# A mixture of experts in a transformer kernel: token rows gathered pair by pair inside the expert loop

## The reference, cut to what matters

```python
# h2 = rms_norm(x) * (1 + sc_f) + sh_f, then for n = 512 tokens:
g_prob = softmax(h @ w_group + b_group);  g_top, g_idx = top_k(g_prob, 1)      # 4 groups
e_prob = softmax(expert logits of that group)                                 # 8 experts in it
e_top, e_idx = top_k(e_prob, 2)
w = g_top * e_top / sum(e_top)                                                # gates of 2 experts a token
for e in range(32):                                                           # D_EXPERT = 256
    a = silu(h @ w_gate_e[e]) * (h @ w_up_e[e])
    y = y + gates[:, e] * (a @ w_down_e[e])
out = x + g_f * y                                                             # then a layer norm
```

## Time and profile before

| | us |
|---|---|
| median of 3 runs (2051.89 to 2058.57) | 2056.76 |
| the profiled execution's own time | 2054.31 |
| its span, first to last instruction | 2052.5 |
| PE busy of the span | 1844.0 (90%) |
| DVE busy | 915.1 (45%) |
| ACT busy | 622.2 (30%) |
| POOL busy | 162.3 (8%) |

### The profile page before, as it was taken

One profiled execution on the slowest core, in us unless ns is written; L12 is line 12 of the kernel. 1 busy time (PEld: TensorE's weight loads), 2 busy tenths in 40 slices (PEclk: granted clock), 3 DMA queues, 4 the chain that ended last, 5 costly groups with the idle time before them and its releaser, 6 DMA issues. The chain is left out here.

```text
span 2052.5 us, 23756 instructions
## 1 busy us (share of the span) xinstructions
PE 1844.0 (90%) x8688; PEld 1262.0 (61%) x8692; DVE 915.1 (45%) x1646; ACT 622.2 (30%) x1121; POOL 162.3 (8%) x239
## 2 busy tenths in 40 slices
PE   4997996587776899999999999988999999999996
PEld 2444644423222556676788878865557678888785
DVE  3787823511102687682322223347866522222234
ACT  2024521110001225742333322223376223333222
POOL 1000000200000242010000000004500100000001
PEclk9999998799888899999999999999999999999998
DMA  9162034499995500032233342250002203334231
GB/s 377 75 246 83 1 126 164 176 420 421 421 422 199 207 1 13 10 119 57 62 102 89 95 143 82 86 196 1 1 22 114 62 23 100 102 94 151 72 93 42
DMA packets 146334, 270.38 MB, mean 132 GB/s; under 512 B 9344, under 2 KB 106624, under 8 KB 132672
## 3 DMA queue, kind: packets, MB, share of 16 engines
q1 hardware_dynamic: 142208, 259.44, 34.9%
q0 software_dynamic: 4032, 9.69, 1.3%
HBM read 260.72 MB, written 13.11 MB: 133 GB/s over the span
## 5 line engine op out<-in xcount | busy, mean ns | idle before, releaser
L278 PE MATMUL bank<-ht_hi,gate_up_hi 128*128 128x512 f32 x704 | 274.1, 389 | 3.1 <-ACT arena L1429 3.1
L280 PE MATMUL bank<-ht_hi,gate_up_lo 128*128 128x512 f32 x704 | 273.9, 389 | 0.0
L279 PE MATMUL bank<-ht_lo,gate_up_hi 128*128 128x512 f32 x704 | 273.9, 389 | 0.0
L2410 PE MATMUL bank<-arena 128*128 128x512 f32 (+3 forms) x640 | 197.1, 467 | 8.2 <-ACT arena L1276 5.6
L2410 PEld LDWEIGHTS bank<-arena 128*128 128x128 f32 x640 | 115.3, 197 | 84.6 <-issue 67.4
L2054 DVE TENSOR_TENSOR arena<-arena,bank 128x512 f32 (+1 forms) x44 | 30.2, 687 | 272.2 <-ACT arena L1295 272.2
L278 PEld LDWEIGHTS bank<-ht_hi,gate_up_hi 128*128 128x128 f32 x704 | 132.1, 188 | 31.3 <-issue 3.9
L280 PEld LDWEIGHTS bank<-ht_hi,gate_up_lo 128*128 128x128 f32 x704 | 132.1, 188 | 27.7
L279 PEld LDWEIGHTS bank<-ht_lo,gate_up_hi 128*128 128x128 f32 x704 | 132.1, 188 | 27.2
L278 PE MATMUL bank<-down_hi,product_hi 128*128 128x512 f32 x352 | 138.2, 393 | 3.5 <-DVE arena L2054 3.5
L280 PE MATMUL bank<-down_hi,product_lo 128*128 128x512 f32 x352 | 138.1, 392 | 0.0
(11 more groups left out here) (373 smaller groups left out, 2938.0 us busy)
## 6 DMA issues: line engine op xcount, KB each, us to landing
gate_up_whole<-w_gu SPq DMA_DIRECT2D x88, 512.0 KB, 5.1
arena<-w_gate_e SPq DMA_DIRECT2D x33, 1024.0 KB, 20.1
arena<-w_up_e SPq DMA_DIRECT2D x33, 1024.0 KB, 23.4
arena<-w_down_e SPq DMA_DIRECT2D x33, 1024.0 KB, 23.2
down_whole<-w_down SPq DMA_DIRECT2D x44, 512.0 KB, 3.5
arena<-w_ada SPq DMA_DIRECT2D x5, 4096.0 KB, 21.2
arena<-w_in SPq DMA_DIRECT2D x4, 2048.0 KB, 16.0
w_o_whole<-w_o SPq DMA_DIRECT2D x2, 4096.0 KB, 13.1
```

What stands on the lines that cost most here:

```text
L278: pe.matmul(ps, xh, wh, start=start, stop=False)
L279: pe.matmul(ps, xh, wl, start=False, stop=False)
L280: return pe.matmul(ps, xl, wh, start=False, stop=stop)
L2410: ins = pe.matmul(ps[:, 0:b - a], HT[:, c, t * P:(t + 1) * P], w_in2[j][:, c], start=c == 0, stop=c == C8 - 1)
```

## The change

It does these things.

- The sorted list goes: no second destination, no eight gathers ahead of the loop, no XsT, no windows. Only the slot layout is left, computed by `mark_places`, and one table (`take_table`) gives, for each slot, its token (`from_token`), its row in `expert_rows` (`to_row`) and its weight (`w_slot`). The table for the 16 pairs is made first; that for the extras inside the loop, at pair 0 (DVE, `extra_rows`) and pair 1 (PE).
- Each pair gathers its own rows from `token_rows` into G (`gather`, two buffers). PE turns them between the gate and up multiplication of the pair before and the turn of A (`turn_rows`, banks 6 and 7); ACT and DVE scale and shift four chunks each into XT (`modulate`).
- The row's weight is put in at the product, the gate row where Y is taken from the banks (`gate_rows`, DVE alone); w_down's result has two banks instead of four. After the loop there is one addition left of the three steps, and nothing for ACT.
- The extras run ahead of pair 9, on the other pair's buffers, stepped by one semaphore `m_extra`; their weights are loaded at pair 6 into slots of their own. The gate and up ring has a sixth slot (used once by expert 5, then by the extras), the w_down ring a fifth (expert 4, then extras). Six and five experts are loaded ahead.
- POOL has more to do ahead of the reciprocal root: two more tables, two shifts and two clears of G.

The core of the diff, with the parts of the loop that the prediction speaks of:

```diff
 CREDIT = 4
-GU_SLOT, DN_RING = [2, 3, 0, 1, 4], 4
-GU_USES_EXTRA, DN_USES_EXTRA = NE // len(GU_SLOT), NE // DN_RING
-GU_AT_EXTRA, DN_AT_EXTRA = (NE - len(GU_SLOT)) // 2, (NE - DN_RING) // 2
+EXTRA_STEPS = 11
+GU_SLOT = [2, 3, 0, 1, 4, 5] + [[2, 3, 0, 1, 4][n % 5] for n in range(NE - 6)]
+DN_SLOT = [0, 1, 2, 3, 4] + [n % 4 for n in range(NE - 5)]
+GU_EXTRA, DN_EXTRA = 5, 4
+ABSENT = 4096
...
+            own.mark(pool.iota(token, [[0, 2], [P, T]], base=-ABSENT, channel_multiplier=1, allow_small_or_imprecise_dtypes=True))
             own.mark(pool.iota(column, [[1, P]], base=0, channel_multiplier=0, allow_small_or_imprecise_dtypes=True))
+            own.mark(pool.iota(column_h, [[1, P]], base=0, channel_multiplier=0, allow_small_or_imprecise_dtypes=True))
+            own.mark(pool.iota(slot_h, [[HALF, NE]], base=0, channel_multiplier=0, allow_small_or_imprecise_dtypes=True))
             own.mark(pool.tensor_copy(ones_b, ones))
             own.mark(pool.tensor_copy(before_b, before_me))
+            own.settle()
+            own.mark(pool.tensor_scalar(column_h, column_h, 0.5 - HALF, None, ALU.add))
+            own.mark(pool.tensor_scalar(slot_h, slot_h, 0.5 - HALF, None, ALU.add))
+            for b in range(2):
+                own.mark(pool.memset(G[b], 0.0))
             own.settle()
             pool.sem_inc(s_count, 1)
             pool.wait_ge(s_ss2, T)
             own.link(pool.tensor_scalar(rstd, ss, 1.0 / D, EPS, ALU.mult, ALU.add))
...
+            def gather(p):
+
+                if p >= 2:
+                    pool.wait_ge(m_xt, p - 1)
+                pool.indirect_dma_start(G[p % 2], None, token_rows, bass.IndirectOffsetOnAxis(from_token[:, p:p + 1], 0),
+                                        bounds_check=last_token, oob_is_err=False).then_inc(s_g[p % 2], 16)
...
+            def scatter(p):
+
+                pool.wait_ge(m_yc, p + 1)
+                pool.indirect_dma_start(expert_rows, bass.IndirectOffsetOnAxis(to_row[:, p:p + 1], 0), Y[:, p % 2], None,
+                                        bounds_check=last_row, oob_is_err=False).then_inc(m_st[p % 2], 16)
+
+            pool.wait_ge(s_tokens, 1)
+            gather(0)
...
             for p in range(EPAIRS):
-                pool.wait_ge(m_ya, p + 1)
-                pool.wait_ge(m_yb, p + 1)
-                pool.indirect_dma_start(expert_rows, bass.IndirectOffsetOnAxis(slots_i[:, p:p + 1], 0), Y[:, p % 2], None,
-                                        bounds_check=last_row, oob_is_err=False).then_inc(m_st[p % 2], 16)
...
+                if p == EXTRA_AT:
+                    pool.wait_ge(s_extra, 2)
+                    apart(pool)
+                    pool.indirect_dma_start(G[2], None, token_rows, bass.IndirectOffsetOnAxis(from_token[:, EPAIRS:EPAIRS + 1], 0),
+                                            bounds_check=last_token, oob_is_err=False).then_inc(s_gx, 16)
+                    scatter(p - 1)
+                    extras = pool.value_load(n_extra[0:1, 0:1], min_val=1, max_val=EXTRAS)
+                    with pool.Fori(0, extras) as x:
+                        own.restart()
+                        pool.wait_ge(m_extra, step(x, 10))
+                        own.mark(pool.tensor_copy(idx_now[:, 0:1], to_row[:, bass.ds(x + EPAIRS, 1)]))
+                        own.mark(pool.tensor_copy(idx_now[:, 1:2], from_token[:, bass.ds(x + EPAIRS + 1, 1)]))
...
+                        pool.wait_ge(s_sx, 16 * (x + 1))
+                        pool.sem_inc(m_extra, 1)
+                    own.settle()
+                elif p:
+                    scatter(p - 1)
+                if p + 1 < EPAIRS and p:
+                    gather(p + 1)
+            scatter(EPAIRS - 1)
...
+            def mark_places(n):
+
+                own.settle()
+                own.link(dve.tensor_tensor(place, OHS, tmp32.unsqueeze(1).broadcast_to([P, 2, T, NE]), ALU.mult))
+                own.link(dve.tensor_reduce(dest_k, place.rearrange("p k t e -> p (k t) e"), AX, ALU.add))
+                own.link(dve.tensor_scalar(tile_k, dest_k, 1.0 / P, ROUND, ALU.mult, ALU.add))
+                own.link(dve.tensor_scalar(tile_k, tile_k, -ROUND, None, ALU.add))
+                own.mark(dve.scalar_tensor_tensor(row_k, tile_k, float(-P), dest_k, ALU.mult, ALU.add))
+                tok, ids, w = (tile_hot[:, :, m * n:(m + 1) * n] for m in range(3))
+                own.link(dve.tensor_tensor(tok, wide_k(tile_k, n), column[:, 0:n].unsqueeze(1).broadcast_to([P, 2 * T, n]), ALU.is_equal))
+                own.mark(dve.tensor_tensor(ids, tok, wide_k(row_ids_k, n), ALU.mult))
+                own.link(dve.tensor_tensor(w, tok, wide_k(wts_k, n), ALU.mult))
+                own.mark(dve.tensor_tensor(tok, tok, wide_k(token_k, n), ALU.mult))
+                own.settle()
+                dve.tensor_tensor(row_hot, wide_k(row_k, P), column_h.unsqueeze(1).broadcast_to([P, 2 * T, P]), ALU.is_equal).then_inc(s_marked, 1)
...
+            def gate_rows(b):
+
+                for half in range(2):
+                    cs = slice(512 * half, 512 * half + 512)
+                    ins = dve.tensor_tensor(Y[:, b, cs], bank[4 + half][:], gate_f[:, cs], ALU.mult)
+                return ins
...
+            dve.wait_ge(m_xt, 1)
+            modulate(0).then_inc(m_xw, 1)
             for p in range(EPAIRS):
                 b = p % 2
...
-                product(p, b)
-                if p + 2 < EPAIRS:
-                    dve.wait_ge(m_gu, p + 1)
-                    window(p + 2)
+                product(b, w_slot[:, p:p + 1]).then_inc(m_a, 1)
+                if p + 1 < EPAIRS:
+                    dve.wait_ge(m_xt, p + 2)
+                    modulate(1 - b).then_inc(m_xw, 1)
+                if p == 0:
+                    extra_rows()
+                if p == 1:
+                    dve.wait_ge(s_tab, 1)
+                    own.mark(take_table(bank[2][:, 2 * P:], EPAIRS, XCOLS, own.mark))
+                    own.settle()
+                    dve.sem_inc(s_extra, 1)
+                dve.wait_ge(m_y, p + 1)
                 if p >= 2:
                     dve.wait_ge(m_st[b], 16 * (p // 2))
-                copy_ya(p, b)
...
+                gate_rows(b).then_inc(m_yc, 1)
...
-                dve.wait_ge(s_w1, t + 1)
-                own.link(dve.scalar_tensor_tensor(Yin[:, t, 0], Yin[:, t, 0], wts[:, t, 0:1], Yin[:, t, 1], ALU.mult, ALU.add))
-                own.link(dve.tensor_tensor(Yin[:, t, 0], Yin[:, t, 0], gate_f, ALU.mult))
+                own.link(dve.tensor_tensor(Yin[:, t, 0], Yin[:, t, 0], Yin[:, t, 1], ALU.add))
...
+            def turn_rows(rows):
+
+                for c in range(C8):
+                    ins = pe.transpose(bank[6 + c // 4][:, c % 4 * P:(c % 4 + 1) * P], rows[:, c::C8], ident)
+                return ins
+
...
-                    pe.sem_inc(m_gfree, 1)
+                if p == 1:
+                    pe.wait_ge(s_marked, 2)
+                    pe.wait_ge(m_atc, 1)
+                    table(bank[2][:, 2 * P:], XCOLS).then_inc(s_tab, 1)
+                if p + 1 < EPAIRS:
+                    pe.wait_ge(s_g[1 - b], 16 * ((p + 1) // 2 + 1))
+                    turn_rows(G[1 - b]).then_inc(m_xt, 1)
+                pe.wait_ge(m_a, p + 1)
                 if p >= 2:
                     pe.wait_ge(m_atc, p - 1)
-                turn_a(p, b)
+                turn_a(b).then_inc(m_at, 1)
...
```

More of the change, by code:

```diff
@@ L195, in plan_first @@
     b.take(("rank",))
-    b.take(("rows",))
-    b.take(("slots",))
-    for g in range(2):
-        for c in range(C8):
-            b.take(("xsT", g, c))
+    b.take(("table",))
     return b
@@ L769, in width, with loads, step @@
             return min(t + 1, 2) * P if kind == "a" else (t + 1) * P
[L771 to L777 removed]
+        def loads(slots, e):
+            s = slots[e]
+            uses = [n for n in range(e) if slots[n] == s]
+            return s, len(uses) + 1, uses[-1] // 2 if uses else None
+        def step(x, n):
+            return (x + 1) * EXTRA_STEPS + n
         def weighted(eng, n):
@@ L989, in _ @@
             pool.wait_ge(s_saved, 16 * T)
-            u1.evacuated(pool, ("rows",))
-            for g in range(2):
-                for q in range(T):
-                    pool.indirect_dma_start(stage[g][:, q], None, token_rows,
-                                            bass.IndirectOffsetOnAxis(row_ids[:, T * g + q:T * g + q + 1], 0)).then_inc(s_stage1 if g else s_stage, 16)
-            u1.evacuated(pool, ("slots",))
-            pool.memset(XsT[:, :, 2 * S:], 0.0).then_inc(s_pad, 1)
-            last_row = pool.to_reg(2 * S - 1)
@@ L1225, in _, with modulate @@
+            def modulate(b):
+                for c in range(C8 // 2):
+                    ins = act.activation(XT[b][:, c], bank[6 + c // 4][:, c % 4 * P:(c % 4 + 1) * P], ACT.Identity,
+                                         bias=mod[:, 2, c:c + 1], scale=mod[:, 3, c:c + 1])
+                return ins
+            act.wait_ge(m_xt, 1)
```

(39 more changed lines are left out.)

467 lines of the change are left out of this document (201 added, 266 removed).

## The result

The changed kernel takes **2100.8 us** (median of 4 runs, 2096.7 to 2102.7); the kernel before, on the same chip, 2056.0. The ratio is 1.0216, with a 95% interval of 1.0196 to 1.0235: slower by 2.2%, 44.8 us. I had predicted 2075, in a range of 2040 to 2090. The sign was right, the size was not. The profiled execution took 2102.67 us (before 2054.31).

What follows compares the result with a forecast made beforehand. It took the loop to be bound by weight loads. Pairs 2 to 14 +15.0, pair 15 -0.3, extra block +2.7, end +0.7: +18.1 on the profiled 2054.3, plus 2.4 to the median, 2075 us; range 2040 to 2090.

Steps and rivals of the forecast that it cites:

- POOL ahead of the root: Ahead of the loop: more POOL work (tables, shifts, clears) before the reciprocal root delays all that follows by 2.9 us.
- Routing to the first multiplication: From the routing counts to PE's first expert multiplication: it comes at 379.3 us instead of 395.44, 16 us earlier.
- The clock charge: Around PE's first expert multiplications: PE at its lower clock after long idling, charged at 2 us.
- Pairs 0 and 1: Start of the loop: the extras' table, 12 us on DVE, delays pair 2's gather; pair 2 starts at 420.4.
- The extra block: Extras ahead of pair 9: hides nothing and takes 18.4 us, against 15.7 behind the loop before.
- Behind the loop: After the expert loop: less work on DVE and ACT, worth nothing, because the next layer waits for w_in.
- The steady pair: Loop pairs 4 to 8 and 10 to 13: 16.8 us a pair on the gather's path, 15.8 before.
- L: In each pair, the gather's time from start to landing: 8.2 us while loads run, 4.4 with idle DMA engines.
- rival B: POOL's queue: the gather also waits for the scatter's rows, L 9.8, 18 us a pair, 2089 to 2093; chance 0.08.
- The averaging: Steady pairs: at 17.5 us the engines run empty and L falls; between 16.2 and 17.5, 16.8 used.
- The constant 9.3: In each pair, all but L: gating, handover, scatter's issue, turns, turn of A, copy and w_down, 9.3 us.
- Rival A: Loop: gathers hide and the weights decide, if L is below 6.9; faster, 2040 to 2048 us; chance 0.26.

Runs made afterwards that it cites:

- run 3: Changed kernel with the gather issued in front of the scatter instead of behind it, still waiting for the same gating event: 2068.6 us in one run.
- Run 4: Changed kernel plus 36 small bf16 multiplications on PE after each gate and up of pairs 2 to 14: 2098.4 us, ratio to before 1.0232.
- run 1: Changed kernel with each gather issued one pair earlier, ahead of the wait for the previous pair's gated rows: 2035.9 us, ratio to before 0.9914.
- Run 2: Changed kernel with the weight loads inside the loop cut from 1024 KB to 128 KB each: 2019.2 us in one run.
- runs 6 and 7: Changed kernel with run 1's edit and the root ahead of POOL's shifts and clears, 2038.3 us; then these held until VectorE's root multiplications are done, 2030.1 us.

## Why the prediction was wrong in size

The path was right: PE waits for the gather in the pairs, the loop's loads set how long, and the loss is made there. The sizes held in front of the loop. *POOL ahead of the root*: VectorE waits 5.88 us instead of 2.88, 3.0 against 2.9. *Routing to the first multiplication*: 377.14 against 379.3; this profile is 2.2 us ahead already at POOL's first iota (326.71, before 328.93), and counted from there it took the 50.4 us that I had predicted. The clock charge was 1.8 us (8.80 instead of 7.04) against 2. *Pairs 0 and 1*: VectorE's block took 11.4 us against 12, pair 2 started at 420.91 against 420.4. Its two ends in VectorE's timeline:

```profile
388.35 0.17 DVE L1777 TENSOR_SCALAR arena<-arena 128x32 f32<-128x32 f32 x1
...
399.70 1.28 DVE L1771 TENSOR_TENSOR arena<-bank,arena 128x512 f32<-128x512 f32 x2
```

That pair 2 and pair 4 (451.0 against 451.5) met their times is in part luck. The gather of pair 2 was issued at 402.60, 3.4 us sooner than I had it, and then took 11.2 us, not 8.6; its turns, the turn of A, the copy and w_down took 7.1 us (413.85 to 420.91), not 5.8. Counted from the first iota pair 2 started 2.7 us late. Pairs 2 and 3 took 17.6 and 12.5 us against 16.3 and 14.8, and these two misses cancel. So what failed later was there in the first gather beside the loads.

*The extra block* took 19.0 us (550.82 to 569.81) against 18.4. *Pair 9*, whose gather found the engines empty (4.1 us), took 14.4 against 14.7, *pair 15* with its last w_down product 12.7 against 12.6, and the rows were read 4.3 us after that, against 4.9. *Behind the loop*: 44.97 us later there, 45.6 at the read; the work saved on VectorE and ScalarE brought nothing.

**The step that failed is "The steady pair".** I used 16.8 us for nine pairs (4 to 8, 10 to 13) and 15.5 for pair 14. Measured: 99.8 us for pairs 4 to 8 (19.96 each), 78.0 for pairs 10 to 13 (19.5 each), 17.15 for pair 14. That is 15.8 + 10.8 + 1.65 = 28.3 us, and the whole miss at the end of the loop is 27.5 (696.29 against 668.8), or 29.7 counted from POOL's first iota. The mechanism was right and three terms of it were mis-sized, L, the averaging and the constant:

- *L.* I took the 8.2 us of a scatter that stands alone in POOL's queue. The gather here stands second. L was 10.0 to 12.2 in six of the ten pairs, and 9.2 on average. That the second one pays is rival B's mechanism, and run 3 shows it: with the order turned round the gather took 8.2 us and the scatter the 2 us more. I had written it down with a chance of 0.08, and with too low a price: 18 us a pair, where 19.5 were measured. It is one of three terms, not the whole miss.
- *The averaging.* I let a pair of 17.5 fall to 16.8 because the engines run empty and L falls. They do, and L falls, but by turns: 14.7 us once, then 20 and more two or three times. That fall is already in the 9.2 us of the average L, so the correction on top of it was not earned. For rival B it hid that 9.3 + 9.8 is 19.1 and not 18.
- *The constant 9.3.* A pair less its L was 10.25 us on average (19.49 - 9.24). The part ahead of the gather's issue was 0.3 us shorter than I had it; the part from the turns to the end of w_down took 7.1 us on average, where I had 5.8. In pair 4 the turns, the turn of A, its copy and w_down took 8.1 us (466.35 to 474.45), in pair 5 5.3 (483.79 to 489.13): that is the lower clock after a long wait (granted clock 0.50 during pair 4's turns, 1.00 during pair 5's). I had put it at nothing in the steady pair. Run 4, with PE kept busy, won back 4.3 us from pair 2 on, and lost some 7 to the fillers in three short pairs; so it neither confirms nor excludes 0.95 us a pair.

By the books of the ten pairs the 28 us are 10.4 for L (9.24 against 8.2), 9.5 for the constant (0.95 a pair), and 8.3 for what I had taken off the 17.5 (0.7 in nine pairs, 2.0 in pair 14). They are not three independent causes: a late gather makes the wait longer, and behind the long waits PE ran at the lower clock.

I also had no term for the bytes of the extras. Their three matrices, 3.1 MB or 7.5 us at 421 GB/s, are loaded in pair 7, so pairs 4 to 8 moved 33 matrices and not 30, with the DMA engines at 0.98. Run 3 shows that this needn't lengthen the pairs: there the same five took 83.6 us and the rest of the bytes moved in the extra block, where the share was 0.89 instead of 0.41. What it added to the landing times here is not shown.

Rival A would have come true with one instruction elsewhere: run 1 lies at 2036, just under A's 2040 to 2048. But its deciding point, L = 6.9, was a property of the order of the code: run 1 has L at 10.2 and hides it all.

What stays open: why the second of two indirect DMAs lands 2 us later and not right behind the first. The Trainium skill ("DMA: Bandwidth & Descriptors", section "Queues, rings and completion order") has each DMA engine change between its queues after a packet; with two requests in one queue, the second one's packets would wait for the first one's turns against the loads too. Run 2 fits it (with light loads both landed in 2.6 to 5.1 us), but no run here separates this from POOL's own work on the descriptors.

## What to carry to other kernels

When a gather moves into a loop, ask first which event its issue waits for, and what stands between it and that event on the issuing engine: here two buffers allowed it to be issued a pair sooner, and the order of two lines decided between 2.2% slower and 0.9% faster. Price a DMA by its place in its own queue as well as by the other traffic: one that goes second needs its own price, even for the same bytes. And when the price depends on how empty the engines are, do not average the states into one pair; follow two or three pairs one after the other.

## What the runs showed of the hardware

- The second of two indirect DMAs of POOL, issued 1.3 us apart beside full loads, takes about 2 us longer from its issue to its landing than the first: 10.0 against 8.0 us (run 3, medians), whichever of gather and scatter it is. Where the loads are thin it doesn't: in six of 13 couples of the changed kernel it took 0.1 to 0.7 us less. With light loads the medians are 4.1 (gather) and 3.1 (scatter).
- VectorE's scaling of four 128x1024 tiles took 4.66 us beside POOL's shifts and clears and 2.74 alone (runs 6 and 7). POOL's shift of 128x128 took 0.99 us there, and 0.57 alone. The Trainium skill ("SBUF — State Buffer", section "SBUF: two separate sides") says that VectorE and GpSimd share one pair of ports, and that beside a GpSimd operation a VectorE one in a two-port mode (or one with two inputs from the buffer, if GpSimd reads it too) has to take turns: the one that comes second blocks until the other's instruction is over. The rows agree in kind; in which mode these operations run no row shows.
- In the changed kernel PE's eight turns ran at the lower of its two clock levels (granted 0.50, 1.97 us) after waits of 5.1 us and more, and at the upper (1.00, 1.16 us) after 1.9 to 3.1 us; after 3.25 us they took 1.52. But the length of the last wait alone doesn't tell it: in run 3, after a wait of 2.70 us, the turns took 1.16 and w_down, 1.9 us later, 5.35 instead of 3.65:

```profile
490.98 1.16 PE L2343 MATMUL bank<-arena 128*128 128x128 f32 x8 [2.70 <-DMA arena<-token_rows,arena]
491.97 0.40 PE L2349 MATMUL bank<-arena 128*128 128x128 f32 x2
492.83 5.35 PE L2411 MATMUL bank<-arena 128*64 128x512 f32 x16 [0.46 <-ACT arena L1248]
```
